# Prompt front and prompt dots of a two-mixer layer with a 16384-expert channel mixer: expert gelus moved on ScalarE, expert selection packed closer on VectorE

## The reference

```
qa ka va qb kb vb f ga gb = rmsnorm(x) @ w_in          # two attention mixers and two gates
m = sigmoid(ga) * (ya @ w_br_a) + sigmoid(gb) * (yb @ w_br_b)
h = x + m @ w_out
q = (rmsnorm(h) @ w_pq)                                 # 8 heads, 2 halves of 128
s = q . sub_keys                                        # 128 scores per head and half
top 16 per half -> 256 candidate sums -> top 16         # 8 heads x 16 = 128 experts per row
a = peer_u[idx] . xn ;  act = gelu(a) * softmax gate
out = h + sum act * peer_v[idx]
```

## Time and profile before

| | |
|---|---|
| median of 3 runs | 2944.23 us (2943.58 to 2946.5) |
| profiled execution | 2943.58 us, its span 2941.7 us |
| PE busy | 2113.0 us, 72% |
| DVE busy | 1909.8 us, 65% |
| POOL busy | 1249.7 us, 42% |
| ACT busy | 471.1 us, 16% |
| gathers (software queue) | 697.85 MB, 59.4% of 16 DMA engines |
| weights and the rest (hardware queue) | 343.97 MB, 32.4% |

### The profile page before, as it was taken

How to read it: one execution, slowest core, us unless ns; L and a number is a source line. 1 busy time by engine, 2 the same in 40 slices (tenths; PEclk the granted TensorE clock), 3 DMA queues, 4 the chain that set the end, 5 groups by cost and what they waited for, 6 DMA issues and landing times.

```text
span 2941.7 us, 19522 instructions
## 1 busy us (share of the span) xinstructions
PE 2113.0 (72%) x6070; PEld 1070.0 (36%) x6070; DVE 1909.8 (65%) x2627; ACT 471.1 (16%) x1104; POOL 1249.7 (42%) x854
## 2 busy tenths in 40 slices
PE   7999999999999887879898820000232027999997
PEld 3665444444545443333344410000231025444443
DVE  1222000276586777566555899999999999666666
ACT  1212000112222110010001000000795025000000
POOL 2000000014254365344434437777777875444444
PEclk9999999999999998999999965555555557999999
DMA  9777688869799999998998969999999997999999
GB/s 343 278 279 255 225 285 306 304 220 392 283 401 381 366 401 413 362 412 350 395 352 346 412 253 397 398 406 392 394 403 399 413 375 245 409 408 408 409 408 361
DMA packets 271465, 1047.11 MB, mean 356 GB/s; under 512 B 19856, under 2 KB 19856, under 8 KB 203280
## 3 DMA queue, kind: packets, MB, share of 16 engines
q0 software_dynamic: 113792, 697.85, 59.4%
q1 hardware_dynamic: 154880, 343.97, 32.4%
q10 hardware_dynamic: 2704, 4.21, 0.4%
HBM read 1036.50 MB, written 9.45 MB: 356 GB/s over the span
## 4 chain that ended last, share of the span: by engine, by line
DVE 26%; DMA 24%; PE 11%; issue 6%; POOL 4%; ACT 0%; POOLq 0%; DVEq 0%; SPq 0%; ACTq 0%
DVE bigr L1538 13%; DMA yTr<-in_peer_v,fold 12%; PE ps L559 10%; DMA bigr<-in_w_br_b 4%; DVE spare L1538 3%; DVE hr L1568 3%; DMA bigr<-in_w_in 3%; POOL bigr L530 2%; DMA bigs<-in_peer_u,idxnow 2%; DMA bigs<-in_peer_v,idxnow 1%; DVE pwork L1349 1%; DMA bigr<-in_w_out 1%; DVE bigs L1477 1%; DVE normed L1558 1%; DVE pwork L1346 0%
## 5 line engine op out<-in xcount | busy, mean ns | idle before, releaser
L559 PE MATMUL ps<-bigr 128*128 128x512 f32 x1920 | 850.2, 601 | 37.3 <-DMA bigr<-in_w_in 21.1
L559 PEld LDWEIGHTS ps<-bigr 128*128 128x128 f32 x1920 | 364.7, 193 | 482.7 <-issue 435.0
L1538 DVE SCALAR_TENSOR_TENSOR bigr<-bigr 128x2048 f32<-128x2048 f32 x213 | 478.1, 2288 | 6.5 <-DMA bigr<-in_peer_u,fold 5.3
L530 POOL DMA_INDIRECT bigr<-in_peer_u,fold x213 | 413.7, 1942 | 130.2 <-DVE bigr L1538 66.8
L489 POOL DMA_INDIRECT bigs<-in_peer_u,idxnow x128 | 216.1, 1688 | 556.1 <-DVE bigs L1487 537.6
L559 PE MATMUL ps<-bigr,bigs 128*128 128x512 f32 x896 | 405.7, 607 | 26.3 <-DMA bigr<-in_w_in 22.6
L1568 DVE SCALAR_TENSOR_TENSOR hr<-yTr,fold,hr 128x1024 f32<-128x1024 f32 x205 | 263.1, 1284 | 129.8 <-DMA yTr<-in_peer_v,fold 127.4
L1487 DVE SCALAR_TENSOR_TENSOR bigs<-bigs 128x2048 f32<-128x2048 f32 x128 | 293.1, 2290 | 82.5 <-DMA bigs<-in_peer_u,idxnow 81.6
L1477 DVE SCALAR_TENSOR_TENSOR bigs<-bigs,acts 128x2048 f32<-128x2048 f32 x128 | 300.9, 2351 | 69.3 <-DMA bigs<-in_peer_v,idxnow 69.2
L540 POOL DMA_INDIRECT yTr<-in_peer_v,fold x205 | 212.6, 1037 | 217.2 <-DVE hr L1568 208.6
L559 PEld LDWEIGHTS ps<-bigr,bigs 128*128 128x128 f32 x896 | 170.3, 195 | 224.2 <-issue 211.7
(11 more groups left out here) (254 smaller groups left out, 2190.0 us busy)
## 6 DMA issues: line engine op xcount, KB each, us to landing
bigr<-in_w_in SPq DMA_DIRECT2D x160, 1024.0 KB, 6.0
spare<-in_peer_v SPq DMA_DIRECT2D x96, 512.0 KB
bigr<-in_w_out SPq DMA_DIRECT2D x32, 1024.0 KB, 9.8
bigr<-in_w_pq SPq DMA_DIRECT2D x32, 1024.0 KB, 8.9
bigr<-in_w_br_a SPq DMA_DIRECT2D x16, 1024.0 KB, 10.3
bigr<-in_w_br_b SPq DMA_DIRECT2D x16, 1024.0 KB
bigr<-in_peer_v SPq DMA_DIRECT2D x32, 512.0 KB
bigr<-in_ckT_a POOLq DMA_DIRECT2D x2, 2048.0 KB, 10.6
```

Of the source, the lines that this page charges most:

```text
L530: pool.indirect_dma_start(ER.urow[k % UBUF], None, a["peer_u"][:, :], bass.IndirectOffsetOnAxis(ap=eidx[t][:, s:s + 1], axis=0)).then_inc( ...
L559: last = mm(ps[:, bank + t, :], src[:, k0 + k, t * P:(t + 1) * P], wring[:, s, k, :], start=(k0 + k == 0), stop=(k0 + k == kt - 1))
L1538: dve.scalar_tensor_tensor(ER.urow[u], ER.urow[u], 1.0, R.xn2[:, t, :], ALU.mult, ALU.mult, accum_out=rdots[:, t, s:s + 1]).then_inc(ER.u_ ...
```

## The change

Three edits, all in the order of code; no instruction is added or taken out.

```
@@ front of ACT, gate pass i
                         for t in range(n):
                             act.activation(F.gate[:, s, t, :], ps[:, 2 * s + t, :], ACT.Sigmoid, scale=scale(t)
                                            ).then_inc(F.proj_read, 1)
-                        experts(PASS_HALVES[0] // 2)
+                        if s == 0:
+                            experts(PASS_HALVES[0])
@@ front of ACT, query projection
                 for i in range(NCH):
+                    if i < 2:
+                        experts(QUERY_HALVES[i])
                     act.wait_ge(piece_done, F.after(PQ + i))
...
-                    experts(QUERY_HALVES[i])
+                    if i >= 2:
+                        experts(QUERY_HALVES[i])
                     keys(i)
@@ DVE, prompt dots
-                if k % 9 in (3, 8) and len(stages) > 1:
+                if k % 3 == 2 and len(stages) > 1:
                     stages.pop(0)()
```

## The result

| | before | after |
|---|---|---|
| median, same chip | 2943.9 us (4 runs, 2942.47 to 2946.5) | 2984.46 us (4 runs, 2973.06 to 2986.5) |
| ratio | | 1.0129, 95% interval 1.0102 to 1.0155 |
| profiled execution | 2943.58 us, span 2941.7 | 2986.50 us, span 2984.6 |

The change is slower, as forecast, but by 41 us and not by 23; the time lies 3.5 us above the upper end of the range. A second chip gave less, 2974.92 us (experiment 5), inside the range. Over both chips the changed kernel ran ten times, from 2967.2 to 2986.5 us with a median of 2979.4, so part of the miss is its spread. The kernel before spreads no less (2937.7 to 2961.7 in 27 runs beside experiments 1 to 4). A single trace therefore carries some us of chance at either kernel.

A forecast was written before the change was run, and what follows sets the result against it. DVE was taken to bound dots covered by selection steps (2.21 us each), transfers the bare ones (2.485 us a row). The sum was 2943.6 + 19 (dots) + 8 (gates) - 4 (query) = 2966.6, predicted 2967 us, range 2952 to 2981.

The forecast's parts named there:

- Dots: 256 prompt dots on DVE: selection steps end earlier, leaving 112 dots bare instead of 40; +19 us, range 16.8 to 22.3.
- a lead of ten: Start of the bare dots: ten run on rows already buffered, so 102 of 112 are paced by transfers, 0.272 us each.
- the bare dots: Dots with no selection step near, behind the covered part; transfers pace them at 2.485 us against 2.21 of DVE.
- Gate pass 0: First prompt gate pass: second sigmoid pair waits for two expert turns; +12.6 us less 5.1 is +7.5, taken as +8.
- the credit: Gate pass 0: two weight pieces not drawn while PE waits bring DVE's gathers up to 5.1 us sooner.
- Not won back in later passes: Gate passes after pass 0: the time lost there is not recovered, even from full buffers.
- Pass 2: Gate pass 2: the later sigmoid pair is covered by PE's 4.99 us wait for weights; cost nothing, otherwise up to 5.
- Query: Query projection: PE waits for a gelu, its lateness is hidden, gathers gain; -4 us, range -5 to +8.
- The two credits: Pass 0 and query projection: weight pieces not drawn speed up gathers, up to 5.1 us in each.
- The first: Rival: gates and query wash out because saturated transfers only swap order, leaving the dots' +19; 2963 us, chance 0.22.
- The second: Rival: PE becomes late; pass 0 costs 12.6, pass 2 or third keys 8, dots without lead 22.3; 2986 us, chance 0.08.
- The third: Rival: transfers limit the whole dot stage, so moving steps is free and query gains 10.2 us; 2933.4 us, chance 0.05.

The follow-up runs named there:

- experiment 5: All three edits together again, on another chip, against the kernel before: 2974.92 us against 2946.5, ratio 1.0098.
- experiment 1: Only the dots edit (a selection step behind every third dot) against the kernel before: 2969.35 us against 2946.66, ratio 1.0077.
- experiment 2: Only the gate edit, in all passes (second sigmoid pair behind both expert gelus), against the kernel before: 2959.44 us, ratio 1.0042.
- experiment 3: Only the query edit (first two query copies behind their expert gelus) against the kernel before: 2945.22 us, ratio 0.9995.
- experiment 4: The gate edit in pass 0 only, passes 1 to 3 as before, against the kernel before: 2963.72 us, ratio 1.0056.
- experiment 9: The gate edit in passes 1 to 3 only, pass 0 as before, against the kernel before: 2946.49 against 2944.64 us, ratio 1.0005.
- experiment 10: The query edit alone, once more, against the kernel before: 2942.63 against 2944.64 us, ratio 0.9990.
- experiment 7: Kernel before with three expert halves moved from the query projection into the output projection: 2921.78 us, ratio 0.9924.

## Why the prediction was right and wrong

**Dots, right.** Forecast +19 from 2.213, 2.485 and a lead of ten; measured +20.6, and +20.4 alone. The part before the bare dots came out at 409.0 us for 408.6. Of the 1.6 us that are off, 0.6 is the working's own 19.6 taken as 19, and 0.5 the lead: eight dots, so 104 paced instead of 102. The rest, 0.5 us, is not assigned. The prediction also said that the transfers sit idle in the covered part; their rate fell (365 GB/s), their share did not (0.96).

**The rule on bandwidth** in the Trainium skill ("DMA: Bandwidth & Descriptors", section "Bandwidth"), 358 GB/s per core on the HBM side, does not agree with the 421 GB/s of the paced dots here either; by it the edit would have cost 52 us. The prediction left out the condition: the same section says that its own measurements, up to 425 GB/s, had the pair's other core idle, and that with both cores streaming each gets roughly 358. This program runs on one core, and its 421 GB/s agree with that.

**Gate pass 0, mis-sized.** This is the step that failed: forecast +8, upper end 12.6; the first sum starts 16.3, 15.8, 11.9 and 17.2 us later in the four traces that have the edit (the changed kernel, experiments 2, 4 and 5). Part of that is how early or late the pass began. From PE's first branch piece to the sum it is 42.1 us before (41.5 to 42.1 in the six other traces with its full weights that leave pass 0 as it was), and 15.2, 14.7, 13.4 and 15.0 us more with the edit. The path to 12.6 was right (gelu, table load, pair, two pieces, DVE). Two things were wrong on it.

First, the credit: "the gathers of DVE's dots come up to 2 x 2.54 = 5.1 us sooner" gave next to nothing. It took two pieces as not drawn while PE stood; but two were on their way, and up to the gelu the weights had moved 0.34 MB less and not 2.1. The dots kept their spacing, 13.75 us for 13.82; from the third to the sixth dot it is 20.1, 20.0, 19.2 and 19.8 us with the edit and 20.0 to 20.3 without, so the credit was 0 to 1 us. What was saved in pieces appears as slack transfers behind the stall (127 GB/s during the last piece), when DVE waits 15.3 us for PE and takes no row.

Second, the clock, a term that the sum did not have: two pieces at a granted clock of 0.67 and then 1.00 took 16.73 us, +2.5 (16.90, 15.72 and 16.84 in the other three traces). In the changed kernel's trace all of pass 0 was also 1.2 us late before the stall (1068.95 for 1067.77). 12.6 + 2.5 + 1.2 = 16.3.

**Not won back in later passes, right**: 331.6 us for passes 1 to 3 in experiment 2, whose ring was full at the start, 333.4 before. It was 334.2 in experiment 4 and 335.5 in experiment 5. Why a full ring buys nothing was not shown. The +5.0 in the changed kernel's trace is no cost of the edit (experiment 9 has none, experiment 1 has +6.0 in unchanged code).

**Pass 2, right**: hidden by the wait for weights, 4.97 us for 4.99.

**Query, the mechanism half wrong.** PE's waits merged and its lateness was hidden, as forecast: keys were ready when DVE asked, and the last key product at 1743.65 held nobody. But DVE's waits for gathers, 20.5 us before, were 20.9 after: the -4 is not in this trace. In experiments 3 and 10 the waits were 2.9 and 0.8 us shorter, and the times of these two leave anything from nothing to -4 open. The credit was again that pieces not drawn go to the gathers. Here 1.50 MB were not drawn, and the gathers moved 0.45 MB more; what kept them from taking more was not shown.

**The sum.** 2943.6 + 20.6 (dots) + 13.4 to 15.2 (pass 0) + 0 (the rest) = 2978 to 2979, beside 2979.4, the median of the changed kernel's ten runs. The two credits took some 9 us off the forecast (4.6 in pass 0, 4 in the query), the clock left out another 2.5, and the dots were 1.6 short; the rest up to 2984.46, some 5 us, lies within the spread and is not assigned. Of the rivals, none described it. The first had pass 0 at nothing. The second came within 2 us of the number, by luck: its 8 us in pass 2 or at the third keys did not come, and its lead of none was eight dots. The third is excluded: transfers ran at 365 GB/s, not 421, in the covered part, and the edit cost 20.6 us.

## What to carry to other kernels

Find for each stage the two rates (here 2.21 us of DVE and 2.485 us of transfers for a row) and spread the extra work of the faster side over all items: each item that runs bare loses the difference, and buffers save only a handful. Before crediting a stalled stream's bandwidth to a neighbour, count what the stalled stream still has on its way (here two pieces, so that 0.34 MB were saved where 2.1 were booked), and do not expect the neighbour to take all that is free (0.45 of 1.50 MB). Work beside a front belongs where its engine waits and transfers have room, and a table of halves moves it there for nothing: that was worth 24.7 us, where none of the changes of order within a stage showed a clear gain.

## What the runs showed of the hardware

The gathers of f32 rows alone reached 421 GB/s on one core, at a DMA share of 1.01. With gathers and a quarter of the weights the share was 0.95 to 0.97 at only 369 to 376 GB/s, and with gathers alone in the covered part 0.96 at 365: share and rate are not the same measure. After 23 us without matmuls PE's granted clock was 0.50, and two pieces took 16.73 us instead of 14.2 to come back from it. In experiment 4, with the same stall, they took 15.72. An issue of a gather took POOL 1.91 us beside dots 2.21 us apart and 2.18 beside dots 2.49 us apart; between the last query copy and the first dot, where DVE runs small steps, it took 0.95 (POOL at 1745.10). Why it stretches was not tested. The changed kernel spreads more from run to run (2967 to 2986 us) than experiment 7 (2919.6 to 2925.4), as does the kernel before (2935.3 to 2949.4 beside experiment 7); what makes that spread was not found.
